# Linear attention: queries scaled in place of states, states in two buffers, and decay gates moved behind the first query chunk

## The reference, cut to what matters

```python
def step(s, xs):                      # gla_chunk_scan, one chunk of 64 tokens
    qc, kc, vc, ac = xs
    b = jnp.cumsum(ac, axis=2)        # ac: log decay, logsigmoid(a @ w_a2 + b_a) / 16
    decay = jnp.exp(jnp.where(mask, b[:, :, :, None, :] - b[:, :, None, :, :], -jnp.inf))
    attn = jnp.einsum('bhid,bhjd,bhijd->bhij', qc, kc, decay)
    o = jnp.einsum('bhid,bhde->bhie', qc * jnp.exp(b), s) + jnp.einsum('bhij,bhje->bhie', attn, vc)
    s_new = jnp.exp(b_last)[..., None] * s + jnp.einsum('bhjd,bhje->bhde', kc * jnp.exp(b_last - b), vc)
    return s_new, o
```

## Time and profile before

| | us |
|---|---|
| median of 3 runs | 2460.51 |
| lowest, highest of the runs | 2457.33, 2462.30 |
| the profiled execution, whole | 2454.73 |
| its span (first to last instruction) | 2452.5 |
| mean granted clock over the span | 0.957 |

### The profile page before, as it was taken

The page is one execution under the profiler, slowest core; times in us unless marked ns, Lnnn a source line. Parts: engine busy times, 40 slices in busy tenths (PEclk is TensorE's granted clock), DMA queues, the critical chain, the costliest instruction groups (busy, mean ns, idle before and its releaser), DMA issues.

```text
span 2452.5 us, 34111 instructions
## 1 busy us (share of the span) xinstructions
PE 2286.6 (93%) x14110; PEld 1851.2 (75%) x14110; DVE 1394.9 (57%) x1999; ACT 576.7 (24%) x1167; POOL 1119.6 (46%) x642
## 2 busy tenths in 40 slices
PE   7999899999899999899999998998988878999998
PEld 5777687887776777687787756697887866788886
DVE  4445578567724444478767762486954664640532
ACT  2043321022232222222022040133534221210210
POOL 5521465765652222465766432163310056556664
PEclk9999999999999999899999999897988979999999
DMA  4210223424421110223433541021110002222321
GB/s 168 86 45 18 69 95 129 154 96 137 151 78 43 44 43 27 83 89 120 153 102 116 184 160 37 14 81 49 65 62 3 3 19 78 78 87 94 108 91 69
DMA packets 55001, 203.84 MB, mean 83 GB/s; under 512 B 6176, under 2 KB 6432, under 8 KB 53568
## 3 DMA queue, kind: packets, MB, share of 16 engines
q1 hardware_dynamic: 52272, 187.28, 23.1%
q0 software_dynamic: 1840, 11.70, 1.3%
q10 hardware_dynamic: 736, 2.69, 0.3%
HBM read 197.45 MB, written 4.19 MB: 82 GB/s over the span
## 4 chain that ended last, share of the span: by engine, by line
PE 87%; DVE 6%; ACT 2%; issue 2%; POOL 2%; DMA 0%; DVEq 0%; SPq 0%; POOLq 0%; ACTq 0%
PE bank L524 65%; PE bank L942 3%; PE bank L970 2%; PE bank L1550 1%; PE bank L1558 1%; PE bank L957 1%; PE bank L2332 1%; POOL parts_r L505 1%; PE bank L1528 1%; PE bank L2596 1%; PE bank L648 1%; PE bank L2328 1%; PE bank L946 1%; PE bank L2317 1%; PE bank L1377 1%
## 5 line engine op out<-in xcount | busy, mean ns | idle before, releaser
L524 PE MATMUL bank<-xn_r,parts_r 128*128 128x512 f32 (+1 forms) x2928 | 922.4, 393 | 33.1 <-DVE mix_r L725 14.3
L524 PE MATMUL bank<-big_r,parts_r 128*128 128x512 f32 x3208 | 935.8, 394 | 16.4 <-DVE big L886 8.9
L499 POOL TENSOR_SCALAR parts_r<-ring 128x1024 fp32r<-128x1024 f32 x293 | 333.3, 1138 | 1057.9 <-PE bank L524 1049.8
L505 POOL TENSOR_TENSOR parts_r<-ring,parts_r 128x1024 fp32r<-128x1024 f32 x293 | 735.9, 2512 | 24.4
L524 PEld LDWEIGHTS bank<-big_r,parts_r 128*128 128x128 f32 x3208 | 605.5, 190 | 149.6 <-DVE big L886 10.6
L524 PEld LDWEIGHTS bank<-xn_r,parts_r 128*128 128x128 f32 x2928 | 554.6, 191 | 153.8 <-issue 32.3
L849 ACT ACTIVATE big<-bank,small 128x512 f32<-128x512 f32 x88 | 68.3, 779 | 419.8 <-DVE big L893 251.3
L878 DVE TENSOR_TENSOR bank<-bank,nb 128x512 f32<-128x512 f32 x88 | 61.3, 699 | 148.8 <-PE bank L524 148.7
L2929 DVE TENSOR_TENSOR big<-big 128x512 f32<-128x512 f32 x32 | 82.6, 2585 | 71.0 <-ACT big_r L2910 71.0
L2855 DVE SCALAR_TENSOR_TENSOR h<-bank,vecs,h 128x512 f32<-128x512 f32 x24 | 17.9, 750 | 173.1 <-PE bank L524 173.1
L535 DVE TENSOR_TENSOR big_r<-big,big_r 128x512 fp32r<-128x512 f32 x76 | 105.6, 1391 | 0.4
(11 more groups left out here) (403 smaller groups left out, 2940.1 us busy)
## 6 DMA issues: line engine op xcount, KB each, us to landing
ring<-weights SPq DMA_DIRECT2D x295, 512.0 KB, 3.5
cst<-mod_w SPq DMA_DIRECT2D x48, 512.0 KB, 4.2
big<-consts POOLq DMA_DIRECT2D x3, 1024.0 KB, 7.6
cst<-consts SPq DMA_DIRECT2D x2, 1280.0 KB, 9.3
h<-x SPq DMA_DIRECT2D x8, 256.0 KB, 7.1
h_store<-h POOLq DMA_DIRECT2D x8, 256.0 KB, 2.3
big<-consts POOLq DMA_DIRECT2D x1, 2048.0 KB, 14.7
h<-h_store POOLq DMA_DIRECT2D x1, 2048.0 KB, 8.2
```

The lines of the kernel that those rows point to most:

```text
L499: pool.tensor_scalar(rounded(unit_parts(u)[0]), ring[:, u % RING], 1.0, 0.0, ALU.mult, ALU.add)\
L505: pool.tensor_tensor(rounded(lo), ring[:, u % RING], value(hi), ALU.subtract).then_inc(part_ready, 1)
L524: mm = pe.matmul(ps, rounded(w[a]), rounded(x[b]), start=(start and n == 0), stop=(stop and n == 2))
```

## The change

Four edits, all in the linear attention:

1. The eight decay-gate products on TensorE stand behind the first query chunk (`fm_multi` gets a hook `then`) and use the banks 4, 5, 6, 7, 2, 3, 4, 5 in place of 0 to 3. `glz_ps` and `glq_ps` get semaphores of their own.
2. VectorE scales queries and keys before it does the gt steps, and waits for the gt steps' signal ahead of its first score mask.
3. `gl_Sr` and its scaling by VectorE go. In its place ScalarE makes scaled queries `gl_q2` once, in 32 copies of 128x64 with a scale column, ahead of its first `gl_U`. `gl_q2` lies where the decays (`gl_b`) lay; the squares for the norm (`gl_sqr`) move to where the scaled keys lay.
4. The state alternates between two buffers: step n reads `gl_S[n % 2]` and writes `gl_S[(n + 1) % 2]`, after cross(n-1) has read it. cross(n) waits once for the state and for `gl_q2`.

The matmuls are the same ones; a cross now has one wait, for the state (`rows`) and the scaled queries. The core of the diff (left out: the lines of the table of signals, ScalarE's wait for `glq_ps`, and parts of the gt steps, which move as they are):

```diff
--- before.py
+++ after.py
...
@@ -782,7 +782,7 @@
                 mod_vectors_dve(dve)
                 rstd_recip(dve, st + "n")
 
-        def fm_multi(pe, name, chunks, parts, full, read, blocks=KD):
+        def fm_multi(pe, name, chunks, parts, full, read, blocks=KD, then=None):
 
             u0 = UNITS[name]
             for f in range(chunks):
@@ -795,6 +795,8 @@
                                            k == 0, k == KD - 1)
                     mm.then_inc(sem(full), 1)
                 product_done[u0 + f] = after(full, (f + 1) * len(parts))
+                if then:
+                    then(f)
 
 
         ff_hi, ff_lo = part(0, KH, T), part(KH * T, KH, T)
@@ -1658,11 +1660,12 @@
         gl_q1, gl_k2 = part(7936, 4, T), part(9984, 4, TA)
         gl_t = gl_k2
         gl_kT = part(13056, NBLK, T)
-        gl_S, gl_Sr = part(16128, 4, GLA_DV), [part(a, 4, GLA_DV) for a in (16512, 18832)]
+        gl_S = [part(a, 4, GLA_DV) for a in (16128, 16512)]
+        gl_q2 = part(4864, 4, T)
         gl_A = part(16896, 2, T)
         gl_sc = part(17920, 3, 4 * NCH)
         gl_U = [part(a, 4, GLA_DV) for a in (18064, 18448)]
-        gl_sqr = part(4864, 4, GW)
+        gl_sqr = part(9984, 4, GW)
         OUTS = ((1, 2), (0, 3))
         out_of = {tb: (p, t) for p, pair in enumerate(OUTS) for t, tb in enumerate(pair)}
 
@@ -1676,20 +1679,24 @@
         gate = mix[:, 5:8].rearrange("p k t -> p (k t)").rearrange("p (b n) -> p b n", b=TB)
         chunks = lambda a: a.rearrange("p (n c) -> p n c", c=CH)
 
+        GLZ_BANKS = (4, 5, 6, 7, 2, 3, 4, 5)
+
         def gates_pe(pe):
             pe.wait_ge(*after("gla_in", 32))
             pe.wait_ge(*after("x2bl", KD))
             fm_multi(pe, "ag", 1, [lat, ctxp], "ag_ps", "ag")
-            pe.wait_ge(*after("ag", 2))
-            for i in range(8):
-                dc, p = divmod(i, 2)
-                d, c = divmod(dc, 2)
-                a, n = ((CTX, T), (0, CTX))[p]
-                ps = grab(pe, i % 4, *after("glz", i + 1))
-                pe.matmul(ps[:, 0:n], gl_w2[32 * d:32 * d + GLA_RANK, c * P:(c + 1) * P],
-                          agT[32 * d:32 * d + GLA_RANK, a:a + n], start=True, stop=True).then_inc(sem("glz_ps"), 1)
-
-            fm_multi(pe, "gl_q", 2, [lat], "glq_ps", "glq")
+
+            def decay_gates():
+                pe.wait_ge(*after("ag", 2))
+                for i in range(8):
+                    dc, p = divmod(i, 2)
+                    d, c = divmod(dc, 2)
+                    a, n = ((CTX, T), (0, CTX))[p]
+                    ps = grab(pe, GLZ_BANKS[i], *after("glz", i + 1))
+                    pe.matmul(ps[:, 0:n], gl_w2[32 * d:32 * d + GLA_RANK, c * P:(c + 1) * P],
+                              agT[32 * d:32 * d + GLA_RANK, a:a + n], start=True, stop=True).then_inc(sem("glz_ps"), 1)
+
+            fm_multi(pe, "gl_q", 2, [lat], "glq_ps", "glq", then=lambda f: decay_gates() if f == 0 else None)
             fm_multi(pe, "gl_k", 2, [lat, ctxp], "glk_ps", "glk")
             tm_linear(pe, "gl_v", GW, lambda k, i: X2_block(k, i), NBLK, "glv_ps", "glv")
             heads_pe(pe, "gla", "gl_g")
...
@@ -1743,7 +1750,7 @@
                 dc, p = divmod(i, 2)
                 a, n = ((CTX, T), (0, CTX))[p]
                 dve.wait_ge(*after("glz_ps", i + 1))
-                dve.tensor_scalar(gl_b[:, dc, a:a + n], bank[i % 4][:, 0:n], gain("gla_b", dc), None, ALU.add)\
+                dve.tensor_scalar(gl_b[:, dc, a:a + n], bank[GLZ_BANKS[i]][:, 0:n], gain("gla_b", dc), None, ALU.add)\
                    .then_inc(sem("glz"), 1)
             dve.wait_ge(*after("glz", 8))
             b, t, d = (a.rearrange("p k t -> p (k t)") for a in (gl_b, gl_t, gl_d))
@@ -1771,20 +1778,6 @@
             dve.tensor_tensor(dcc, bc, sc[:, 0].unsqueeze(2).broadcast_to((P, 4 * NCH, CH)), ALU.subtract)\
                .then_inc(sem("gla_diff"), 1)
 
-            dve.wait_ge(*after("gt_ln", 1))
-            link(dve, dve.scalar_tensor_tensor(out=z, in0=z, scalar=0.0, in1=az, op0=ALU.max, op1=ALU.add))
...
-            link(dve, dve.tensor_scalar(z[0:32], z[0:32], is_bwd[64:96], None, ALU.mult))
-            dve.scalar_tensor_tensor(out=g[0:32], in0=az[0:32], scalar=is_fwd[64:96], in1=z[0:32], op0=ALU.mult,
-                                     op1=ALU.add).then_inc(sem("gt"), 1)
             dve.wait_ge(*after("gla_diff", 1))
             dve.wait_ge(*after("glq", 2))
             dve.wait_ge(*after("glk", 4))
@@ -1796,6 +1789,21 @@
             dve.wait_ge(*after("gla_en", 1))
             for dc in range(4):
                 dve.tensor_tensor(gl_k2[:, dc], gl_k[:, dc % 2], gl_d[:, dc], ALU.mult).then_inc(sem("gla_qk"), 1)
+
+            dve.wait_ge(*after("gt_ln", 1))
+            link(dve, dve.scalar_tensor_tensor(out=z, in0=z, scalar=0.0, in1=az, op0=ALU.max, op1=ALU.add))
+            dve.wait_ge(*after("ea", 1))
+            link(dve, dve.tensor_scalar(z, z, column(vecs, 136)[64:P], None, ALU.mult))
+            link(dve, dve.tensor_copy(g, z))
+            dve.wait_ge(*after("gla_in", 32))
+
...
+                                     op1=ALU.add).then_inc(sem("gt"), 1)
 
 
         def steps(d):
@@ -1850,11 +1858,13 @@
                 for d in range(2):
                     c = steps(d)[n] - CCH
                     r = CH * (c % 2)
-                    pe.wait_ge(sem("gl_Sr"), 2 * (n - CCH) + d + 1)
+                    if d == 0:
+                        pe.wait_ge(*after("gl_S", n))
+                        pe.wait_ge(sem("gl_q2"), 1)
                     for hd in (0, 2, 1, 3):
                         q, dc = 64 * (hd % 2), 2 * d + hd // 2
-                        mm = pe.matmul(gl_out(c // 2, hd, slice(r, r + CH)), gl_q1[q:q + 64, dc, c * CH:(c + 1) * CH],
-                                       gl_Sr[(n - CCH) % 2][q:q + 64, dc, :], start=False,
+                        mm = pe.matmul(gl_out(c // 2, hd, slice(r, r + CH)), gl_q2[q:q + 64, dc, c * CH:(c + 1) * CH],
+                                       gl_S[n % 2][q:q + 64, dc, :], start=False,
                                        stop=(hd >= 2 and n in last_cross))
                     mm.then_inc(sem("gl_x"), 1)
 
@@ -1879,6 +1889,12 @@
                 act.wait_ge(*after("gl_turn", b + 1))
                 act.activation(gl_kT[:, b], bank[2 + b % 2][:, :], ACT.Copy).then_inc(sem("glkT"), 1)
             act.wait_ge(*after("gla_esc", 1))
+            act.wait_ge(*after("gla_qk", 4))
+            for dc in range(4):
+                for c in range(NCH - CCH):
+                    ins = act.activation(gl_q2[:, dc, c * CH:(c + 1) * CH], gl_q1[:, dc, c * CH:(c + 1) * CH], ACT.Copy,
+                                         scale=gl_sc[:, 0, dc * NCH + CCH + c:dc * NCH + CCH + c + 1])
+            ins.then_inc(sem("gl_q2"), 1)
             for n in range(NCH - 1):
                 act.wait_ge(*after("gl_U", n + 1))
                 if n >= 2:
@@ -1891,6 +1907,7 @@
 
         def gla_dve(dve):
             v4 = lambda a: a.rearrange("p (h n) -> p h n", h=GH)
+            dve.wait_ge(*after("gt", 1))
             for tb in range(TB):
 
                 dve.wait_ge(*after("gl_s", 2 * tb + 2))
@@ -1905,27 +1922,17 @@
                 link(dve, ins)
                 dve.tensor_tensor(A, A, B_, ALU.add).then_inc(sem("gl_A"), 1)
             dve.wait_ge(*after("gla_esc", 1))
-            scol = lambda kind, d, c: gl_sc[:, kind].rearrange("p (a n) -> p a n", a=4)[:, 2 * d:2 * d + 2, c:c + 1]\
-                .broadcast_to((P, 2, GLA_DV))
-            for n in range(NCH):
+            for n in range(NCH - 1):
                 m = n - CCH
-                if m >= 0:
-                    if m >= 2:
-                        dve.wait_ge(*after("gl_x", 2 * m - 2))
-                    for d in range(2):
-                        dve.tensor_tensor(gl_Sr[m % 2][:, 2 * d:2 * d + 2], gl_S[:, 2 * d:2 * d + 2],
-                                          scol(0, d, steps(d)[n]), ALU.mult).then_inc(sem("gl_Sr"), 1)
-                if n == NCH - 1:
-                    break
+                if m >= 1:
+                    dve.wait_ge(*after("gl_x", 2 * m))
                 dve.wait_ge(*after("gl_u", n + 1))
-                if m >= 0:
-                    dve.wait_ge(sem("gl_Sr"), 2 * m + 2)
                 if n == 0:
-                    dve.tensor_copy(gl_S, gl_U[0]).then_inc(sem("gl_S"), 1)
+                    dve.tensor_copy(gl_S[1], gl_U[0]).then_inc(sem("gl_S"), 1)
                 else:
                     for dc in range(4):
                         c = steps(dc // 2)[n]
-                        ins = dve.scalar_tensor_tensor(out=gl_S[:, dc], in0=gl_S[:, dc],
+                        ins = dve.scalar_tensor_tensor(out=gl_S[(n + 1) % 2][:, dc], in0=gl_S[n % 2][:, dc],
                                                        scalar=gl_sc[:, 1, dc * NCH + c:dc * NCH + c + 1],
                                                        in1=gl_U[n % 2][:, dc], op0=ALU.mult, op1=ALU.add)
```

28 lines of the change are left out of this document (14 added, 14 removed).

## The result

The changed kernel takes 2445.98 us (median of 5 runs, 2442.93 to 2451.86), the kernel before 2460.51: ratio 0.9943, interval 0.9923 to 0.9963, so 9 to 19 us less.

What follows compares the result with a forecast made beforehand. TensorE holds 87% of the chain, with VectorE setting the recurrence's pace. Gains of 4.4 (stretch to the values) + 0 + 0 + 3.3 (recurrence) = 7.7 us take 2460.51 to 2452.8; range 2447 to 2457.

Steps and rivals of the forecast that it cites:

- The local sum: Linear attention: 4.4 from the stretch to the values plus 3.3 from the recurrence, 7.7 us gained.
- No wait, and a clean first query chunk: From `ag` to the values: TensorE goes on at once; at 2.4 GHz the stretch is 33.9 us, 8.3 less.
- (b): Gate block and following query chunk: a clock fall inside the block is likely and costs 3.9 us (ends 0 and 5.8).
- (a): First key chunk's second part: TensorE waits 0.6 us for ScalarE's second query copy, if the clock is high.
- The gates' own time: Eight gate products behind the first query chunk: 2 x 2.84 us at 2.4 GHz, 5.68 in all.
- Edit 2 at 0, ends 0.7: VectorE's scaling ahead of gt steps costs 0; effects of collisions with POOL taken as 0, ends 0.7 us either way.
- Rival D: Ahead of the first mask: VectorE's gt steps become the path, kernel slower, 2467.8 us; chance 0.05.
- Turns and scores at no change: Between values and recurrence: no gain counted; the clock's course, scores included, left open by some 2 us.
- ScalarE's 32 copies hidden: Ahead of ScalarE's first `gl_U`: copies at 0.27 each take 8.6 us of idle time, cost 0, upper end 0.8.
- Recurrence 3.3: Delta-rule recurrence: without VectorE's 0.63 scaling, steps of 1.60 then 1.15 us gain 3.3 (ends 1.6 and 5.3).
- Rival B: Gate block: the clock does not fall, gain 7.7 + 3.3 = 11.0 us, so 2449.5; chance 0.28.

Runs made afterwards that it cites:

- e_pairs: Changed kernel with the gate products of the two directions issued by turns; ratio to the kernel before 0.9946.
- e_gates: Kernel before with edit 1 alone: gate products behind the first query chunk, in the new banks; ratio to the kernel before 0.9964.
- e_recur: Kernel before with edits 3 and 4 alone: queries scaled by ScalarE, two state buffers; ratio to the kernel before 0.9978.
- e_gt_first: Changed kernel with edit 2 undone: gt steps ahead of the scaling again; ratio to the kernel before 0.9946.
- e_banks: Kernel before with gate products in their old place but in banks 4, 5, 6, 7, 2, 3, 4, 5; ratio to the kernel before 0.9994.
- e_one_state: Changed kernel with one state buffer, each state step waiting for the cross that reads it; ratio to the kernel before 0.9984.
- e_gates_twice: Changed kernel with each of the eight gate products issued twice; a single run, 2457.08 us.
- e_warm: Changed kernel with unread small 128-row products on TensorE between the score products and in the first recurrence steps; ratio to the kernel before 0.9940.
- e_best: Changed kernel with e_gt_first, e_pairs, e_warm and ScalarE's second query copy between Exp and Ln; 2433.96 us, ratio to the kernel before 0.9912.

## Why the prediction was right in kind and wrong in size

The local sum was 7.7; the profile has 13.4. The mechanism was right, and the terms that were off are sizes: the clock's price, the gates' own time and TensorE's step at the low clock were put too high; edit 2, put at nothing, costs time. By the prediction's own steps:

- **No wait, and a clean first query chunk** (33.9 at a high clock): right. From the end of `ag` to the gates there are 5.36 us, 5.44 expected.
- **(b), the clock's price, is the term that failed: 3.9, measured 1.8.** That the clock falls in or behind the gates was right: it did in every kernel here that has the products one direction after the other, in ten of twelve profiles; only in the two with pairs it did not. But I took the price from one event, a fall *ahead of* four products; it stayed low through them and 6 us of query matmuls. With the fall 0.8 us behind the block, the chunk behind it took 7.3 in place of 5.44, and the gates themselves lost nothing.
- **(a), the stall of 0.6 without a fall:** as foreseen it was not there in after; without a fall it is 1.82 (e_pairs), since VectorE's last reading ended 2.1 us behind the gates and not 0.7.
- **The gates' own time: 5.68 taken, 4.2 measured.** I doubled the 2.84 of the earlier trace rows. It is the products of one direction, and at the seam the last of direction 1 and the first of direction 2 ran at once; e_pairs shows it for all of them (3.3). 1.5 us more gain.
- **Edit 2 at 0, ends 0.7: wrong, it costs 1.9** against either kernel that does without it, and 0.8 against the kernel before, which had one such wait itself. I had said that the wait for POOL would probably go, and it does once edit 1 moves VectorE against TensorE (e_gates); moving the gt steps beside the output gate's splits brings it back twice, 0.82 and 0.89, where I had put 0.3 to 0.5 each and netted it to nothing. The reason is where the slow splits fall: a pair of them beside the gt steps took 4.90 us (1642.77 to 1647.67), a unit of the values leaves 6.24 for it (1627.09 to 1633.33 on POOL), a unit of the output gate 4.16 (1637.30 to 1641.46 before the change). The order buys nothing in return, as the scaling is in time without it: in e_gates it ends at 1647.0, as the turns start at 1647.3. Rival D's mechanism did not show: 7.68 us idle ahead of the first mask.
- **Turns and scores at no change: 1.6 less, by luck.** The clock fell later in them in this profile (1666.1 for a first turn at 1652.0). Over the profiles the length of this stretch follows the fall: 22.06 to 22.34 where it came 8.5 to 8.8 us behind the first turn (e_gates, e_recur, e_gt_first, e_pairs), 21.40 to 21.50 at 9.5 to 10.3 (before, e_banks, e_one_state, e_gates_twice), 19.78 at 14.1 (after), 18.27 and 17.92 with no fall (e_warm, e_best). It is no gain to count on. The prediction had left 2 us open for it.
- **ScalarE's 32 copies hidden:** right, 0.24 each.
- **Recurrence 3.3, measured 4.6.** The parts as the crosses show them: first cross 0.45 earlier, seven steps in 8.80 in place of 12.39, so 3.6 (I had 2.5), last cross 0.6 shorter. Two numbers were off, against each other. TensorE's 1.60 at the low clock was the old step less the 0.17 of idle in the earlier trace rows; it still held the effect of the two waits in a cross, whose sixteen records start over 0.82 us before the change and over 0.58 after, at the same clock. With one wait the step is 1.37 to 1.48, and only the first step here lay wholly at the low clock. At the high clock I had 1.15; the six steps behind the first took 7.43, 1.24 each, with the 1.98 among them. The recurrence came out at 15.6 to 15.9 in six kernels, whenever the clock rose.

7.7 + 2.1 (clock) + 1.5 (gates) - 0.8 (POOL) + 1.6 (scores) + 1.3 (recurrence) = 13.4. The timed difference, 9 to 19 us, holds it, and e_gt_first's 12.8 and e_pairs' 12.0 as well; a value nearer 12 is what these kernels have in common. All errors but one had the same sign: I had priced the clock and TensorE's step by their worst rows, and the 1.6 of the scores is luck. Rival B gave 11.0 for the wrong reason (no fall), and was still short.

The rule of the Trainium skill (TensorE: Matmul & The Clock Gate, section "HAM oscillation — how this bites in real kernels") that idle gaps make the clock fall does not hold by itself here: e_gates_twice fell with TensorE busy in each slice. Its advice in the section "Why this matters for your kernels", to put small products into separate groups of rows so that they run at once, the profiles agree with: 3.3 us for the block against 4.2.

## What to carry to other kernels

A clock that falls has a place and a cause: find what TensorE ran ahead of it, busy or not, and price a move of that work by the length of the low time that it will have in its new place, not in its old. A low clock also hides other engines' lateness; when it goes, look for the next wait (1.82 and 1.79 here) and move that engine's work in the same step. And before a step of the slowest engine in a ring is taken out, check that its buffer is not what let the others run ahead: one buffer cost 7.2 us against two here, with the clock low, and two gave 4.6 against the kernel before.

## What the runs showed of the hardware

- Products over 16 rows of the array, back to back and with TensorE busy in each slice, did not keep the clock in e_gates_twice: it fell 5.1 us into a block of 14.3, and did not rise in the 9.3 left of it; it rose 4.4 us after full 128-row products had begun. In the six kernels with the single block behind the first query chunk, one direction after the other, it fell 0.4 to 1.0 us behind the block. Ahead of the falls in the scores TensorE ran products over 64 rows, and had also waited up to 2.05 us for VectorE; with small 128-row products in those waits there was no fall (e_warm, e_best). What exactly the chip counts was not tried.
- Two products over 16 rows each, in rows 0 to 15 and 32 to 47, run at once: eight in 3.3 us, against 4.2 where only those at the seam overlap.
- POOL's splits beside VectorE's operations: 2.95 for the subtraction and 1.87 for the rounding beside the gt steps, against 2.40 and 1.05 alone. It is two waits of 0.8 to 0.9 for TensorE. The 5.61 of the earlier trace rows started with a VectorE operation of 3.36 us, both at 1618.79, and is 3.21 longer than a split alone.
- The part of the kernel that is the same in all of them ended anywhere from 1564 to 1576 us. Of a change of this size one profile's whole span says little.
